# Fourth small expert in the mixture-of-experts stage of a two-layer decoder, and the order of its eight jobs

## The chip, the cores and the metric

The kernel runs on one core of a Trainium2 chip. Its engines are TensorE (PE in the profile; PEld is its weight load), VectorE (DVE), ScalarE (ACT), GpSimd (POOL) and SyncE (SP), each with its own instruction stream, joined by semaphores. The metric is the device time of one execution in microseconds (us); lower is better.

## The reference, cut to what matters

Two layers run on 256 tokens of 1024 numbers, all in float32. Layer 0 is retention and a dense SwiGLU, layer 1 is block attention and a top-2-of-8 mixture of experts (MoE). The change is in the MoE alone:

```python
def moe_swiglu(x, router, w_in, w_out):
    B, T, D = x.shape
    xt = x.reshape(B * T, D)
    logits = (xt @ router).astype(jnp.float32)
    top_v, top_i = lax.top_k(logits, MOE_TOP_K)
    top_w = jax.nn.softmax(top_v, axis=-1)
    gates = jnp.sum(jax.nn.one_hot(top_i, N_EXPERTS, dtype=jnp.float32) * top_w[..., None], axis=1)
    out = jnp.zeros_like(xt)
    for e in range(N_EXPERTS):
        out = out + gates[:, e:e + 1].astype(x.dtype) * swiglu(xt, w_in[e], w_out[e])
    return out.reshape(B, T, D)
```

Each expert has an input matrix of 1024 x 7168 (gate and up halves of 3584) and an output matrix of 3584 x 1024, in all 42 MB of 1024 x 1024 bytes. With the reference's inputs, its router gives experts 0 to 7 the following numbers of tokens: 60, 61, 58, 57, 89, 66, 54, 67 (sum 512).

## The kernel before

A float32 product is made of products of a high part and a low part (float32r, a shorter mantissa): x = hi + lo. ACT writes the high part of each weight tile (`moe_hi`, L834), DVE subtracts it from the tile and writes the low part (`moe_lo`, whose subtraction is L964 of `lo_of`), and PE multiplies.

The MoE works in eight **jobs**, one an expert, and each job in 42 **units** of 1 MB of weights (128 partitions x 2048 numbers). SP loads the units in order into eight buffers (six of `raw`, two of `more_raw`), a load waiting until `moe_lo` of eight units earlier is done (L498). ACT and DVE write the two parts into four buffer pairs (`whi`/`wlo` three, `whi_more`/`wlo_more` one), each waiting until PE has used the unit of four earlier. ACT and DVE programs are written out by hand, four units ahead of PE's: `moe_hi(n+4)`, `moe_lo(n+4)` stand in the turn of unit n, beside the activations and copies of that turn.

A job first needs its tokens. They are gathered by a product of h with a 0/1 matrix `sel` (made on POOL, `select`), and the result is added back with the transposed matrix (`turn_sel` at unit 6 of a job; `scatter` at units 2 and 4 of the next job, after which DVE adds it into h, L1323). There are two forms of a job:

- **Big** (`big_unit`): up to 128 tokens. The tokens' hi and lo parts are two separate stationary operands of 128 columns (`xg_big`), and each weight tile is swept three times: hi x hi, hi x lo, lo x hi (L1422, L1423, L1424). A unit has 12 matmuls of 512 columns.
- **Small** (`small_unit`): up to 64 tokens. The hi and lo parts of 64 tokens stand side by side in one stationary operand of 128 columns (`xg_small`), and each tile is swept twice: with the hi weights and with the lo weights (L1842, L1843). A unit has 8 matmuls of 512 columns. The two halves are added by a product with `merge` (L1879, `turn_merged`), and there are row copies on ACT (L860, L865).

Expert 0 is always first. The other seven are sorted by their number of tokens, from most to least, and get positions 1 to 7 (`sort_experts`). `POSITION` says which position runs as which job. Positions 5, 6 and 7 are small, so the forms of jobs 0 to 7 are big, small, big, small, big, small, big, big. The tokens of jobs 2m+1 and 2m+2 are gathered together in job 2m, in eight steps (`gather_pair`, units 13 to 31; a step is four matmuls, L1759), each copied by ACT before the next (`copy_gathered`). Job 6 gathers for job 7 alone.

If an expert has more tokens than its capacity (128 for a big one, 64 for a small one), `see_excess` sets `over`, and after the eight jobs eight more big jobs run for the rest (`more > 0`).

POOL loads the last norm's parameters (`ln_last`, 2 x 512 KB) when the last unit of job 6 is used (L619). After the last job, `drain_y`, `scatter`, the two adds into h and the last layer norm end the kernel.

Of the kernel before, what the change touches and what calls it, by code (L numbers as in the profile page):

```python
# [7 lines left out]
ACT = mybir.ActivationFunctionType  # L8
# [6 lines left out]
P = 128  # L15
# [14 lines left out]
def build(nc, x, ln_g, ln_b, ret_w_in, ret_gn_g, ret_gn_b, ret_w_out, kv_w, moba_w_q, moba_w_out,  # L30
# [3 lines left out]
    KD = D // P  # L34
# [10 lines left out]
    EX = moe_router.shape[2]  # L45
# [14 lines left out]
    JOBS = EX  # L60
# [8 lines left out]
    assert EFF == 3 * W + BANK and len(BIG_STREAM) == len(SMALL_STREAM) == JOB_UNITS and U_MOE % SPLIT == 0 and JOB_UNITS % RAW == 0  # L69

    HALF = P // 2
    POSITION = [0, 5, 1, 6, 2, 7, 3, 4]
    SMALL = [position >= 5 for position in POSITION]
    BIGS, SMALLS = SMALL.count(False), SMALL.count(True)
    CAPACITY = [P] * 5 + [HALF] * 3
    FIRST_KEY = 1 << 14
    assert not SMALL[0] and not SMALL[-1]

    BIG_SILU = {3: (0, 0), 4: (0, 1), 11: (1, 0), 12: (1, 1), 23: (2, 0), 24: (2, 1), 33: (3, 0)}
    BIG_MUL = {7: (0, 0), 8: (0, 1), 19: (1, 0), 20: (1, 1), 31: (2, 0), 32: (2, 1), 35: (3, 0)}  # L80
# [37 lines left out]
    with ctx:  # L118
        def sem(name):
            return ctx.enter_context(nc.semaphore(name))  # L120
# [4 lines left out]
        def place(name, shape, dt=F32, at=None):  # L125

            size = (math.prod(shape[1:]) * 4 + 31) // 32 * 32
            line = ALIGN if size >= ALIGN else 32
            start = (map_at[0] + line - 1) // line * line if at is None else at
            assert start + size <= nc.sbuf_usable_end, name  # L130
            if at is None:
                map_at[0] = start + size
            return nc.alloc_sbuf_tensor_at(name, shape, dt, offset=start), start
# [46 lines left out]
        capacity, _ = place("capacity", [P, EX])  # L180
        key_limit, _ = place("key_limit", [P, EX])
# [21 lines left out]
        xg_big = [place(f"xg_big{i}", [P, KD, 2, P], F32R, at=xT_at + i * 8192)[0] for i in range(2)]  # L203
# [3 lines left out]
        xg_small, _ = place("xg_small", [P, KD, P], F32R)  # L207
# [11 lines left out]
        sel, _ = place("sel", [P, 2, T, 2 * P], F32R)  # L219
# [25 lines left out]
        ps = ctx.enter_context(nc.psum_tensor("ps", [P, 8, BANK], F32))  # L245
# [66 lines left out]
        moe_tables = sem("moe_tables")  # L312
# [8 lines left out]
        gathered = sem("gathered")  # L321
        big_copied = sem("big_copied")
        small_copied = sem("small_copied")
# [108 lines left out]
        def bigs_before(j):  # L432
            return SMALL[:j].count(False)

        def smalls_before(j):
            return SMALL[:j].count(True)

        def sel_of(j):

            if j == 0:  # L440
                return sel[:, 1, :, 0:P]
            c = P if SMALL[j] else 0
            return sel[:, (j - 1) // 2 % 2, :, c:c + P]
# [4 lines left out]
        def _(sp):  # L448
# [47 lines left out]
            def moe_unit(u, i, e, slot, dst, free, small=False):  # L496
                src, rows = moe_source(i, e, small)
                sp.wait_ge(lo_done, free)  # L498
                sp.dma_start(dst.rearrange("p (k n) -> p k n", k=rows), src).then_inc(landed[slot], 16)

            def expert(position):
                return sp.value_load(expert_at[0:1, position:position + 1].bitcast(I32), min_val=0, max_val=EX - 1)

            for j in range(JOBS):
                if j == 0:
                    e = 0
                else:
                    if j == 1:
                        sp.wait_ge(experts_sorted, 1)
                    e = expert(POSITION[j])  # L510
                for i in range(JOB_UNITS):
                    n = j * JOB_UNITS + i
                    if n == RAW:
                        sp.wait_ge(h_ready, T * 2 + 1)
                    back = MRAW if n >= MRAW else RAW
                    moe_unit(U_MOE + n, i, e, moe_slot(n), moe_raw(n), U_MOE + n - back + 1 if n < RAW or n >= MRAW else U_MOE,
                             SMALL[j])

# [17 lines left out]
        def _(pool):  # L536
# [49 lines left out]
            for t in range(T):  # L586
# [4 lines left out]
            pool.tensor_tensor(merge[:, :], ident[:, 0:HALF], ident[:, HALF:P], ALU.add).then_inc(moe_tables, 1)  # L591
            pool.iota(key_low[:, :], pattern=[[-1, EX]], base=EX - 1, channel_multiplier=0,
                      allow_small_or_imprecise_dtypes=True).then_inc(moe_tables, 1)
            pool.memset(capacity[:, 0:5], float(P)).then_inc(moe_tables, 1)
            pool.memset(capacity[:, 5:EX], float(HALF)).then_inc(moe_tables, 1)
            pool.memset(key_limit[:, 0:1], float(FIRST_KEY + EX * (P + 1))).then_inc(moe_tables, 1)
            pool.memset(key_limit[:, 1:5], float(EX * (P + 1))).then_inc(moe_tables, 1)
            pool.memset(key_limit[:, 5:EX], float(EX * (HALF + 1))).then_inc(moe_tables, 1)
            pool.wait_ge(moe_tables, 8)
            pool.memset(key_low[:, 0:1], float(FIRST_KEY + EX - 1)).then_inc(moe_tables, 1)  # L600
            for n in (1, 2):
# [11 lines left out]
            for q in range(4):  # L613
                if q >= 1:
                    pool.wait_ge(selT_done, 2 * q - 1)
                for t in range(T):
                    for j in range(2 * q + 1, min(2 * q + 3, JOBS)):
                        select(q, t, SMALL[j], POSITION[j])
            pool.wait_ge(unit_used, first_unit(JOBS - 1))  # L619
# [4 lines left out]
        def _(act):  # L624
# [76 lines left out]
            for i in range(PIECES):  # L701
                w = slice(i * UNIT // PIECES, (i + 1) * UNIT // PIECES)
# [13 lines left out]
            for s in range(12):  # L716
                u, c = U_RET_IN + QK_UNITS + 4 + s, 2 + s // 2
# [172 lines left out]
            def copy_gathered(j, k):  # L890

                step = j // 2 * KD + k
                w = P if j + 2 >= JOBS else P + HALF
                src = ps[:, 7, 0:2 * w].rearrange("p (s n) -> p s n", s=2)
                act.wait_ge(gathered, step + 1)
                nc.scalar.activation(xg_big[(bigs_before(j) + 1) % 2][:, k, :, :], src[:, :, 0:P],
                                     ACT.Copy).then_inc(big_copied, 1)
                if w > P:
                    nc.scalar.activation(xg_small[:, k, :].rearrange("p (s n) -> p s n", s=2), src[:, :, P:w],
                                         ACT.Copy).then_inc(small_copied, 1)  # L900

            def drain_y(u):
                unit_done(act, u + JOB_UNITS - 1, 0)
# [30 lines left out]
            with act.If(more > 0):  # L934
                with act.Fori(0, JOBS) as p:
                    for k in range(KD):
                        act.wait_ge(gathered, 4 * KD + k + 1 + KD * p)
                        nc.scalar.activation(xg_big[0][:, k, :, :].rearrange("p s n -> p (s n)"), ps[:, 7, 0:2 * P],
                                             ACT.Copy).then_inc(big_copied, 1)
                    copy_selT(JOBS + p)  # L940
                    for i in range(AHEAD):
                        again_hi(p, i)
                    for i in range(JOB_UNITS):
                        again_hi(p, i + AHEAD)
                        big_drains(i, U_AGAIN + JOB_UNITS * p, BIGS + p)
                    drain_y(U_AGAIN + JOB_UNITS * p)
# [7 lines left out]
        def _(dve):  # L954
# [360 lines left out]
            def place_gates():  # L1315

                then(to_positions(gate_of[:, :, 1:1 + EX], gate_expert))
                then(nc.vector.tensor_copy(gate_of[:, :, 0:1], gate_of[:, :, 1 + POSITION[-1]:2 + POSITION[-1]]))

# [44 lines left out]
            for j in range(JOBS):  # L1364
                u = first_unit(j)
                for i in range(JOB_UNITS):
# [11 lines left out]
                    else:  # L1378
                        if i == 0:
                            drain_y(j - 1)  # L1380
                        elif i in (3, 5):
                            t, at = i // 5, 1 + POSITION[j - 1]
                            dve.wait_ge(h_scaled, T)
# [35 lines left out]
        def _(pe):  # L1419
# [335 lines left out]
            def gather_step(k, dst, chosen, w):  # L1755

                for s, src in enumerate((h_hi, h_lo)):
                    for t in range(T):
                        last = pe.matmul(dst[:, s * w:(s + 1) * w], src[:, t, k * P:(k + 1) * P], chosen[:, t, 0:w],  # L1759
                                         start=(t == 0), stop=(t == T - 1))  # L1760
                return last

            def gather_pair(j, k):

                w = P if j + 2 >= JOBS else P + HALF
                if k == 0:
                    pe.wait_ge(selT_ready, j + 1)
                    pe.wait_ge(sel_ready, min(2 * T * (j // 2 + 1), T * (JOBS - 1)))
                else:
                    pe.wait_ge(big_copied, j // 2 * KD + k)  # L1770
                    if w > P:
                        pe.wait_ge(small_copied, j // 2 * KD + k)
                gather_step(k, ps[:, 7, :], sel[:, j // 2 % 2], w).then_inc(gathered, 1)

            def turn_sel(job, chosen):

# [172 lines left out]
            with pe.If(more > 0):  # L1949
                with pe.Fori(0, JOBS) as p:  # L1950
                    pe.wait_ge(selT_ready, JOBS + p)
                    pe.wait_ge(y_lo_done, 2 * JOBS + 2 * p)
                    for t in range(T):
                        scatter(t)
                        pe.wait_ge(summed, T * (JOBS - 1) + t + 1 + T * p)
                    pe.wait_ge(sel_again, T + T * p)
                    for k in range(KD):
                        gather_step(k, ps[:, 7, :], sel[:, 0], P).then_inc(gathered, 1)
                        pe.wait_ge(big_copied, 4 * KD + k + 1 + KD * p)
                    turn_sel(JOBS + p, sel[:, 0, :, 0:P])  # L1960
                    big = BIGS + p
                    for i in range(JOB_UNITS):
                        big_unit(i, U_AGAIN + JOB_UNITS * p, big, JOBS + p, xg_big[0], whi[:, i % SPLIT, :],
                                 wlo[:, i % SPLIT, :], (big_silu, 7 * big),
                                 (big_mul, 7 * big))
                        big_turn(i, big)
# [26 lines left out]
```

## Time and profile before

| | |
|---|---|
| time, median of 3 runs | 1469.05 us (1467.59 to 1470.61) |
| the profiled execution | 1468.5 us |
| its span in the profile | 1466.7 us, so 1.8 us lie around the span |
| PE, DVE, ACT busy | 97%, 78%, 66% of the span |
| the MoE's eight jobs | from about 540 us to the end |

Each row of a grouped view tells a line of the code, the engine, the operation, output and inputs with shapes, the number of instructions, their busy time and mean duration, and the idle time ahead of them with what ended it. Matmuls overlap, so one of 0.39 us starts every 0.23 us; intervals between starts are what counts. In the view of busy time by stretch a row gives the stretch and its length in us, then busy time and number of instructions of PE, PEld, DVE, ACT and POOL, PE's granted clock (1.00 is full), the DMA engines' busy share and the rate in GB/s. In a row of a timeline stand start, duration, engine, line and operation, and in brackets the idle time before it and what ended it. In a row of DMA issues the last number is the median time from issue to landing in us.

### The profile page before, as it was taken

How to read it: one execution, taken by the hardware profiler on the slowest of the kernel's cores; microseconds unless marked ns; L12 is line 12 of the kernel's file. 1: busy time of each engine (PE TensorE's matmuls, PEld its weight loads, DVE VectorE, ACT ScalarE, POOL GpSimd, SP SyncE). 2: the span in 40 equal slices, each digit the busy share in tenths (PEclk: the TensorE clock that was granted, in tenths of full speed). 3: DMA queues.
4: the chain of work that ended last, by engine and by line, in shares of the span. 5: the costliest groups of instructions: out<-in, count | busy, mean ns of one | idle time of the engine just before them, and what ended most of it. 6: DMA issues, size and time to landing. Idle time of an engine off the chain costs nothing.

```text
span 1466.7 us, 18711 instructions
## 1 busy us (share of the span) xinstructions
PE 1423.2 (97%) x7478; PEld 1207.5 (82%) x7478; DVE 1142.5 (78%) x795; ACT 961.6 (66%) x796; POOL 55.7 (4%) x66
## 2 busy tenths in 40 slices
PE   9999999999999999999999999999999999999996
PEld 9987789999889887887778887778887778888885
DVE  5456564545556598899998888999888999889886
ACT  5334544343444477778987777987777997777774
POOL 2001200000000021000002000001000000000000
PEclk9999999999999999999999999999999999999999
DMA  9654556555564469999999999999999999999990
GB/s 361 214 172 149 202 173 209 187 182 190 172 202 147 136 249 364 359 355 370 417 420 420 377 358 346 404 420 420 382 357 351 395 420 420 398 358 379 378 343 30
DMA packets 158743, 446.89 MB, mean 305 GB/s; under 512 B 7088, under 2 KB 46000, under 8 KB 158656
## 3 DMA queue, kind: packets, MB, share of 16 engines
q1 hardware_dynamic: 156832, 439.38, 80.5%
q0 software_dynamic: 1824, 6.33, 1.2%
q8 instruction: 57, 0.93, 0.2%
q14 instruction: 30, 0.25, 0.0%
HBM read 444.63 MB, written 1.05 MB: 304 GB/s over the span
## 4 chain that ended last, share of the span: by engine, by line
PE 73%; DVE 22%; ACT 2%; issue 2%; POOL 0%; DVEq 0%; ACTq 0%; POOLq 0%
PE ps L1422 21%; PE ps L1424 21%; PE ps L1423 21%; DVE wlo L964 13%; DVE wlo_more L964 4%; PE ps L1842 1%; PE ps L1843 1%; PE ps L1836 1%; PE ps L1759 1%; ACT whi L834 1%; PE ps L1879 1%; DVE h L1323 1%; DVE wlo L387 1%; PE ps L1468 1%; DVE y_lo L964 1%
## 5 line engine op out<-in xcount | busy, mean ns | idle before, releaser
L964 DVE TENSOR_TENSOR wlo<-raw,whi 128x2048 fp32r<-128x2048 f32 (+1 forms) x214 | 480.0, 2257 | 53.6 <-ACT whi L834 52.9
L834 ACT ACTIVATE whi<-raw 128x2048 fp32r<-128x2048 f32 x208 | 397.3, 1917 | 104.2 <-PE ps L1424 95.8
L387 DVE TENSOR_TENSOR wlo<-raw,whi 128x2048 fp32r<-128x2048 f32 x80 | 184.1, 2302 | 154.8 <-ACT whi L380 154.8
L380 ACT ACTIVATE whi<-raw 128x2048 fp32r<-128x2048 f32 x82 | 156.8, 1912 | 152.4 <-PE ps L1424 151.3
L1422 PE MATMUL ps<-whi,xg_big 128*128 128x512 f32 x420 | 166.1, 395 | 0.5 <-DVE wlo L964 0.5
L1424 PE MATMUL ps<-whi,xg_big 128*128 128x512 f32 x420 | 163.9, 390 | 0.0
L1423 PE MATMUL ps<-wlo,xg_big 128*128 128x512 f32 x420 | 163.7, 390 | 0.0
L1422 PE MATMUL ps<-xT_hi,whi 128*128 128x256 f32 x576 | 163.3, 284 | 0.0
L1424 PE MATMUL ps<-xT_hi,wlo 128*128 128x256 f32 x576 | 163.0, 283 | 0.0
L1423 PE MATMUL ps<-xT_lo,whi 128*128 128x256 f32 x576 | 163.0, 283 | 0.0
L1422 PEld LDWEIGHTS ps<-xT_hi,whi 128*128 128x128 f32 x576 | 110.5, 192 | 0.5
L1423 PEld LDWEIGHTS ps<-xT_lo,whi 128*128 128x128 f32 x576 | 110.5, 192 | 0.4
L1424 PEld LDWEIGHTS ps<-xT_hi,wlo 128*128 128x128 f32 x576 | 110.5, 192 | 0.0
L964 DVE TENSOR_TENSOR wlo<-more_raw,whi 128x2048 fp32r<-128x2048 f32 x42 | 96.1, 2287 | 12.3 <-ACT whi L834 12.3
L1842 PE MATMUL ps<-whi,xg_small 128*128 128x512 f32 x252 | 99.7, 396 | 2.8 <-DVE wlo L964 2.3
L834 ACT ACTIVATE whi_more<-more_raw 128x2048 fp32r<-128x2048 f32 x42 | 80.6, 1918 | 32.9 <-PE ps L1424 20.8
L964 DVE TENSOR_TENSOR wlo_more<-more_raw,whi_more 128x2048 fp32r<-128x2048 f32 x42 | 96.0, 2286 | 7.5 <-ACT whi_more L834 7.2
L834 ACT ACTIVATE whi_more<-raw 128x2048 fp32r<-128x2048 f32 x42 | 80.5, 1917 | 31.3 <-PE ps L1424 20.7
L964 DVE TENSOR_TENSOR wlo_more<-raw,whi_more 128x2048 fp32r<-128x2048 f32 x42 | 96.0, 2287 | 6.0 <-ACT whi_more L834 6.0
L1843 PE MATMUL ps<-wlo,xg_small 128*128 128x512 f32 x252 | 98.3, 390 | 0.0
L834 ACT ACTIVATE whi<-more_raw 128x2048 fp32r<-128x2048 f32 x42 | 80.5, 1917 | 18.8 <-PE ps L1424 17.6
L1422 PEld LDWEIGHTS ps<-whi,xg_big 128*128 128x128 f32 x420 | 79.0, 188 | 16.7 <-issue 1.7
(253 smaller groups left out, 2750.7 us busy)
## 6 DMA issues: line engine op xcount, KB each, us to landing
raw<-in_moe_w_in SPq DMA_DIRECT2D x166, 1024.0 KB, 6.9
raw<-in_moe_w_out SPq DMA_DIRECT2D x86, 1024.0 KB, 7.8
more_raw<-in_moe_w_in SPq DMA_DIRECT2D x58, 1024.0 KB, 7.0
more_raw<-in_moe_w_out SPq DMA_DIRECT2D x26, 1024.0 KB, 7.7
raw<-in_ret_w_in SPq DMA_DIRECT2D x23, 1024.0 KB, 6.8
raw<-in_ffn_w_in SPq DMA_DIRECT2D x22, 1024.0 KB, 4.9
raw<-in_ffn_w_out SPq DMA_DIRECT2D x11, 1024.0 KB, 4.8
raw<-in_ret_w_out SPq DMA_DIRECT2D x8, 1024.0 KB, 4.9
```

Of the source, the lines that this page charges most:

```text
L380: nc.scalar.activation(whi[:, u % SPLIT, :], src, ACT.Copy).then_inc(hi_done, 1)
L387: nc.vector.tensor_tensor(wlo[:, u % SPLIT, :], src, whi[:, u % SPLIT, :].bitcast(F32), ALU.subtract).then_inc(lo_done, 1)
L834: nc.scalar.activation(moe_split(n)[0], moe_raw(n), ACT.Copy).then_inc(hi_done, 1)
L964: return nc.vector.tensor_tensor(dst, src, hi.bitcast(F32), ALU.subtract)
L1323: nc.vector.scalar_tensor_tensor(out=h[:, t, :], in0=ps[:, at:at + 2, :].rearrange("p b n -> p (b n)"), scalar=gate, in1=h[:, t, :], op0=A ...
L1422: pe.matmul(dst, a_hi, b_hi, start=start, stop=False, skip_group_check=True)
L1423: pe.matmul(dst, a_hi, b_lo, start=False, stop=False, skip_group_check=True)
L1424: return pe.matmul(dst, a_lo, b_hi, start=False, stop=stop, skip_group_check=True)
L1468: pe.matmul(ps[:, at, 3 * P:4 * P], ident[:, :], ident[:, :], start=True, stop=True)
L1759: last = pe.matmul(dst[:, s * w:(s + 1) * w], src[:, t, k * P:(k + 1) * P], chosen[:, t, 0:w], start=(t == 0), stop=(t == T - 1))
L1842: pe.matmul(dst, a, hi, start=start, stop=False, skip_group_check=True)
L1843: return pe.matmul(dst, a, lo, start=False, stop=stop, skip_group_check=True)
```

## The change

Four positions (4 to 7) are small instead of three, and the jobs alternate: `POSITION` is now 0, 4, 1, 5, 2, 6, 3, 7, so that the forms are big, small, big, small, big, small, big, small. Jobs 0 to 6 have the forms that they had; job 7 is now small. Job 1 takes the expert of position 4 instead of 5, job 3 that of 5 instead of 6, job 5 that of 6 instead of 7, and job 7 that of position 7 (the fewest tokens) instead of 4. The gather of job 6 is for 64 slots alone, and ACT copies it to `xg_small` alone; steps wait on `small_copied` only. The tables of capacities and limits follow, and the overflow jobs' constants too.

```diff
-    POSITION = [0, 5, 1, 6, 2, 7, 3, 4]
-    SMALL = [position >= 5 for position in POSITION]
+    POSITION = [0, 4, 1, 5, 2, 6, 3, 7]
+    FIRST_SMALL = 4
+    SMALL = [position >= FIRST_SMALL for position in POSITION]
     BIGS, SMALLS = SMALL.count(False), SMALL.count(True)
-    CAPACITY = [P] * 5 + [HALF] * 3
...
-            pool.memset(capacity[:, 0:5], float(P)).then_inc(moe_tables, 1)
-            pool.memset(capacity[:, 5:EX], float(HALF)).then_inc(moe_tables, 1)
+            pool.memset(capacity[:, 0:FIRST_SMALL], float(P)).then_inc(moe_tables, 1)
+            pool.memset(capacity[:, FIRST_SMALL:EX], float(HALF)).then_inc(moe_tables, 1)
...
             def copy_gathered(j, k):
                 step = j // 2 * KD + k
-                w = P if j + 2 >= JOBS else P + HALF
+                w = HALF if j + 2 >= JOBS else P + HALF
                 src = ps[:, 7, 0:2 * w].rearrange("p (s n) -> p s n", s=2)
                 act.wait_ge(gathered, step + 1)
-                nc.scalar.activation(xg_big[(bigs_before(j) + 1) % 2][:, k, :, :], src[:, :, 0:P],
-                                     ACT.Copy).then_inc(big_copied, 1)
-                if w > P:
-                    nc.scalar.activation(xg_small[:, k, :].rearrange("p (s n) -> p s n", s=2), src[:, :, P:w],
-                                         ACT.Copy).then_inc(small_copied, 1)
+                if w > HALF:
+                    nc.scalar.activation(xg_big[(bigs_before(j) + 1) % 2][:, k, :, :], src[:, :, 0:P],
+                                         ACT.Copy).then_inc(big_copied, 1)
+                nc.scalar.activation(xg_small[:, k, :].rearrange("p (s n) -> p s n", s=2), src[:, :, w - HALF:w],
+                                     ACT.Copy).then_inc(small_copied, 1)
...
             def gather_pair(j, k):
-                w = P if j + 2 >= JOBS else P + HALF
+                c, w = (P, HALF) if j + 2 >= JOBS else (0, P + HALF)
                 if k == 0:
                     pe.wait_ge(selT_ready, j + 1)
                     pe.wait_ge(sel_ready, min(2 * T * (j // 2 + 1), T * (JOBS - 1)))
                 else:
-                    pe.wait_ge(big_copied, j // 2 * KD + k)
-                    if w > P:
-                        pe.wait_ge(small_copied, j // 2 * KD + k)
-                gather_step(k, ps[:, 7, :], sel[:, j // 2 % 2], w).then_inc(gathered, 1)
+                    pe.wait_ge(small_copied, j // 2 * KD + k)
+                gather_step(k, ps[:, 7, :], sel[:, j // 2 % 2, :, c:c + w], w).then_inc(gathered, 1)
```

## Rows read from the trace of the kernel before

**Rows 1.** The page's first part: span, busy time by engine.
```profile
span 1466.7 us, 18711 instructions
PE 1423.2 (97%) x7478; PEld 1207.5 (82%) x7478; DVE 1142.5 (78%) x795; ACT 961.6 (66%) x796; POOL 55.7 (4%) x66
```
**Rows 2.** Timeline of PE: the transposes of `sel` (L1778) of jobs 1 to 7.
```profile
672.72 0.38 PE L1778 MATMUL ps<-ident,sel 128*128 128x128 f32 x2
...
775.09 0.38 PE L1778 MATMUL ps<-ident,sel 128*128 128x128 f32 x2
...
900.48 0.38 PE L1778 MATMUL ps<-ident,sel 128*128 128x128 f32 x2
...
1002.88 0.38 PE L1778 MATMUL ps<-ident,sel 128*128 128x128 f32 x2
...
1127.03 0.38 PE L1778 MATMUL ps<-ident,sel 128*128 128x128 f32 x2
...
1229.42 0.38 PE L1778 MATMUL ps<-ident,sel 128*128 128x128 f32 x2
...
1352.80 0.38 PE L1778 MATMUL ps<-ident,sel 128*128 128x128 f32 x2
```
**Rows 3.** Busy time by stretch (job 5, job 7): columns as told above.
```profile
1105.40:1207.30 101.90, 96.54 (x459) 77.21 (x457) 98.18 (x54) 89.36 (x67) 0.00 (x0) 0.98 1.01 390
...
1332.10:1451.80 119.70, 119.70 (x543) 98.69 (x541) 102.33 (x58) 82.72 (x56) 1.11 (x2) 1.00 0.79 301
```
**Rows 4.** Timeline of DVE: job 5's last low part, job 6's first.
```profile
1202.80 2.28 DVE L964 TENSOR_TENSOR wlo_more<-raw,whi_more 128x2048 fp32r<-128x2048 f32 x1
1205.00 4.48 DVE L964 TENSOR_TENSOR wlo<-raw,whi 128x2048 fp32r<-128x2048 f32 x2
```
**Rows 5.** Timeline of PE: last unit of job 5, end of job 7.
```profile
1205.13 0.50 PE L1842 MATMUL ps<-whi_more,gT_small 128*128 128x512 f32 x1
...
1206.86 0.39 PE L1843 MATMUL ps<-wlo_more,gT_small 128*128 128x512 f32 x1
...
1451.43 0.39 PE L1424 MATMUL ps<-whi_more,gT_lo 128*128 128x512 f32 x1
```
**Rows 6.** Timeline of PE: second scatters of jobs 1, 3, 5.
```profile
666.22 0.50 PE L1785 MATMUL ps<-y_hi,selT 128*128 128x512 f32 x1 [2.90 <-DVE h L1323]
...
891.15 0.80 PE L1785 MATMUL ps<-y_hi,selT 128*128 128x512 f32 x1 [2.89 <-DVE h L1323]
...
1118.96 0.64 PE L1785 MATMUL ps<-y_hi,selT 128*128 128x512 f32 x1 [2.89 <-DVE h L1323]
```
**Rows 7.** Chain that ended last: gather steps of jobs 4, 6.
```profile
1023.30 0.42 PE ps L1759 x4
1023.72 0.25 PE ps L1422
...
1249.84 0.40 PE ps L1759 x4
1250.23 0.28 PE ps L1422
```
**Rows 8.** DMA issues at 1120 to 1130, 1200 to 1210, 1333 us; last: landing.
```profile
raw<-in_moe_w_in SPq DMA_DIRECT2D x1, 1024.0 KB, 7.6
...
raw<-in_moe_w_in SPq DMA_DIRECT2D x5, 1024.0 KB, 12.4
...
ln_last<-in_ln_b POOLq DMA_DIRECT2D x1, 512.0 KB, 9.5
```
**Rows 9.** Busy time by stretch: two short stretches of job 5.
```profile
1130.00:1140.00 10.00, 10.00 (x53) 8.36 (x51) 9.24 (x6) 9.25 (x9) 0.00 (x0) 1.00 0.96 336
1190.00:1200.00 10.00, 9.46 (x40) 6.78 (x38) 10.00 (x7) 9.37 (x6) 0.00 (x0) 1.00 1.02 420
```
**Rows 10.** Timeline of ACT: job 5's last high part, job 6's second.
```profile
1198.15 1.90 ACT L834 ACTIVATE whi_more<-raw 128x2048 fp32r<-128x2048 f32 x1
...
1202.60 1.92 ACT L834 ACTIVATE whi<-raw 128x2048 fp32r<-128x2048 f32 x1 [0.28 <-DMA raw<-in_moe_w_in]
```

More of the change, by code:

```diff
@@ L71, in build @@
     HALF = P // 2
-    POSITION = [0, 5, 1, 6, 2, 7, 3, 4]
-    SMALL = [position >= 5 for position in POSITION]
+    POSITION = [0, 4, 1, 5, 2, 6, 3, 7]
+    FIRST_SMALL = 4
+    SMALL = [position >= FIRST_SMALL for position in POSITION]
     BIGS, SMALLS = SMALL.count(False), SMALL.count(True)
-    CAPACITY = [P] * 5 + [HALF] * 3
     FIRST_KEY = 1 << 14
-    assert not SMALL[0] and not SMALL[-1]
+    assert not SMALL[0] and SMALL[-1]
     BIG_SILU = {3: (0, 0), 4: (0, 1), 11: (1, 0), 12: (1, 1), 23: (2, 0), 24: (2, 1), 33: (3, 0)}
@@ L593, in _ @@
                       allow_small_or_imprecise_dtypes=True).then_inc(moe_tables, 1)
-            pool.memset(capacity[:, 0:5], float(P)).then_inc(moe_tables, 1)
-            pool.memset(capacity[:, 5:EX], float(HALF)).then_inc(moe_tables, 1)
+            pool.memset(capacity[:, 0:FIRST_SMALL], float(P)).then_inc(moe_tables, 1)
+            pool.memset(capacity[:, FIRST_SMALL:EX], float(HALF)).then_inc(moe_tables, 1)
             pool.memset(key_limit[:, 0:1], float(FIRST_KEY + EX * (P + 1))).then_inc(moe_tables, 1)
-            pool.memset(key_limit[:, 1:5], float(EX * (P + 1))).then_inc(moe_tables, 1)
-            pool.memset(key_limit[:, 5:EX], float(EX * (HALF + 1))).then_inc(moe_tables, 1)
+            pool.memset(key_limit[:, 1:FIRST_SMALL], float(EX * (P + 1))).then_inc(moe_tables, 1)
+            pool.memset(key_limit[:, FIRST_SMALL:EX], float(EX * (HALF + 1))).then_inc(moe_tables, 1)
             pool.wait_ge(moe_tables, 8)
@@ L936, in _ @@
                     for k in range(KD):
-                        act.wait_ge(gathered, 4 * KD + k + 1 + KD * p)
+                        act.wait_ge(gathered, JOBS // 2 * KD + k + 1 + KD * p)
                         nc.scalar.activation(xg_big[0][:, k, :, :].rearrange("p s n -> p (s n)"), ps[:, 7, 0:2 * P],
@@ L1958, in _ @@
                         gather_step(k, ps[:, 7, :], sel[:, 0], P).then_inc(gathered, 1)
-                        pe.wait_ge(big_copied, 4 * KD + k + 1 + KD * p)
+                        pe.wait_ge(big_copied, (BIGS - 1) * KD + k + 1 + KD * p)
                     turn_sel(JOBS + p, sel[:, 0, :, 0:P])
```

## The prediction

> **What bounds the kernel now.** I read the page's first part, then the busy time by stretch, then the timelines of PE and DVE at the ends of a small and of a big job. The first part gives PE as busy in 97% of the span [rows 1], which says little alone, since overlapping matmuls count as busy. The stretches tell the jobs apart. In job 7, which is big, PE is busy all of 119.7 us and DVE 102.3 of them: PE sets the pace [rows 3]. In job 5, which is small, DVE is busy 98.2 of 101.9 us and PE 96.5: DVE is the fuller engine [rows 3]. The end of job 5 shows it. DVE starts its last low part at 1202.80 and the next one at 1205.00, 2.20 us a unit, and PE starts the last unit at 1205.13, at once when that part is written; the eight matmuls' starts lie between 1205.13 and 1206.86, so PE needs about 2.0 us for a unit and waits for DVE [rows 4, 5]. So a small job is no third shorter, as its 8 matmuls for 12 would have it: it is cut off by the splitting of the weights. What it costs has to be read from the three small jobs that run already.
>
> The transposes of `sel` at unit 6 are the milestones [rows 2]. From a small job's to that of the big job behind it it is 102.37, 102.40 and 102.39 us (jobs 1, 3, 5). From a big job's to that of the small job behind it, it is 125.39 (job 2) and 124.15 us (job 4). From job 6 to job 7, big to big, it is 123.38 us.
>
> **The change part by part.** All is compared with the profiled run, whose span is 1466.7 us and whose time is 1.8 us more, 1468.5; that is 0.55 under the median of 1469.05.
>
> (a) Jobs 0 to 6, up to unit 6 of job 6 at 1229.42 us. Their forms, unit streams and gathers are the same, and which expert stands at a small position changes only addresses of loads and a column of `slot_of` and `gate_of`. The memsets of two tables have other widths on POOL, long before they are read. Price 0.
>
> (b) Job 7's own units. From its transpose to the start of its last matmul job 7 takes 1451.43 - 1352.80 = 98.63 us [rows 2, 5]. Job 5, small, takes 1206.86 - 1127.03 = 79.83 us for the same units [rows 2, 5]. Difference: -18.80 us. It may be carried over because in job 5 the low parts of the next job's units come behind the low part of unit 41 on DVE (the one of 1205.00 is job 6's first), so they delay nothing of job 5 itself; in the last job they are absent, and nothing else is in their place. The high part of unit 41 started at 1198.15, on ACT, 4.6 us before the low part needed it [rows 4, 10], so ACT doesn't set this end either.
>
> (c) The way into job 7. With a small job behind job 6 the interval from transpose to transpose is that of job 4 or 2, not 123.38 us. It falls in two. From the big job's transpose to the second scatter it is 116.06 us (775.09 to 891.15) and 116.08 us (1002.88 to 1118.96) [rows 2, 6], so it can be trusted. There PE waited 2.9 us for DVE's add into h, in all three small jobs, since DVE has low parts queued ahead of the add [rows 6]. From the scatter to the small job's transpose it is 6.50, 9.33 and 8.07 us in jobs 1, 3 and 5 [rows 2, 6]: the first matmul is at 0.50 us in job 1, and at 0.80 and 0.64 in the others, where PE's granted clock had fallen to its lower level, 1.2 GHz, for some matmuls after that wait. The way in is 116.07 plus one of the three: 122.57, 124.14 or 125.40 us. Against 123.38 that is -0.81, +0.76 or +2.02. I take the middle one, +0.8, as the value of the nearest small job in time, and keep both ends.
>
> (d) The gather of job 6. Its eight steps are four matmuls each, now of 64 columns instead of 128; jobs 0, 2 and 4, whose intervals I used in (c), have 192. With 192 columns a step takes 0.42 us and the matmul behind it 0.25; with 128 columns it takes 0.40 and 0.28 [rows 7], 0.67 and 0.68 in sum. A third fewer columns bring nothing, so the step is at a floor that the columns don't set. For 64 columns no row exists. Upper end: the same, 0. Lower end: halving from 128 in proportion to columns, -0.20 us a step or -1.6 us in all. I take 0, because the step from 192 to 128 brought 0. Copies on ACT in job 6: one to `xg_small` instead of one to `xg_big`, a smaller one; ACT is not what PE waits for in a big job (PE is busy without a gap in such a one [rows 3]), so 0. PE's new wait in steps 1 to 7 is for that copy on ACT instead of the bigger one; what is queued behind it on PE is the next unit, and the steps lie two units or more apart, 5 us, so it is met.
>
> (e) Moved with it: the load of `ln_last` (1 MB in all on POOL's queue), issued when job 6 ends. Until now it fell into a big job's slack, now it falls into a small job, where loads are issued at DVE's faster pace. In job 5 the loads took 7.6 us to land at its start and 12.4 at its end, and the rate rose from 336 to 420 GB/s [rows 8, 9]: they were falling behind. ACT first waited for a load at job 6's unit 1 (0.28 us, at 1202.60), two units behind the last of job 5's own [rows 10]. In the last job there is no unit behind unit 41, so this wait can't come. The extra 1 MB is 2.5 us at 420 GB/s; at the start the loads run 84 GB/s under that rate, which gives back 0.8 MB in each 10 us, so it should be taken in by 20 to 30 us into the job. Price 0, with an end of +2.5 us if it isn't. The landing itself (9.5 us for the second half [rows 8]) is needed only some 100 us later.
>
> (f) The end. `drain_y`, the scatters, the adds and the norm are as before: 1466.7 - 1451.43 = 15.27 us behind the start of the last matmul [rows 1, 5]. DVE and ACT are free at that point as before. Price 0.
>
> The Trainium skill holds something against all this. Its page "DMA: Bandwidth & Descriptors", section "Where 436 GB/s comes from", says that for transfers between HBM and SBUF the HBM side binds, at about 358 GB/s for a core. As an estimate from that page, a job's 44.04 MB would need 123 us, a small job could not be shorter than a big one, and the change would give nothing. The trace disagrees: job 5 ran at 390 GB/s over its whole length and at 420 in its last part [rows 3, 9].
>
> **The sum.** -18.8 (b) + 0.8 (c) = -18.0 us. The span becomes 1448.7 us, the time 1450.5; set against the median instead of the profiled run, 1451.05 us. I give 1451.0.
>
> **The rivals.**
> 1. *The load stream falls behind in the last job.* For it: landings stretch to 12.4 us in job 5, and 1 MB more is put into this one [rows 8]. Against it: job 5's own last high part met no late load [rows 10]. It gives the sum plus up to 2.5 us: 1453.5 us.
> 2. *A small job at the end is worth nothing*, because the stream or DVE needs as long for its 42 units as PE does for a big one. It would be so if a job's bytes could come no faster than in about 120 us; the price is the whole of (b), and the way in stays: about 1470 us. Against it: three small jobs that run in 102.4 us [rows 2], which include all their loads.
> 3. *Slower: the overflow runs.* Position 4 now has 64 slots instead of 128. From 65 tokens on at that position, eight more big jobs run. Each costs at least the big-to-big interval, 123.4 us [rows 2], in all some 990 us: about 2440 us. By the tokens of the reference's inputs expert 0 (60) is fixed, and the other seven in order are 89, 67, 66, 61, 58, 57, 54. Position 4 is the fourth of these, 61 tokens, three under the limit. So it decides only if the inputs were others, or if the kernel's arithmetic moved four tokens.
>
> **How the numbers follow.** Forecast 0.86, rival 1 0.10, rival 2 0.02, rival 3 0.02. Range: down from 1451.0 by 1.6 (a way in without a fallen clock) and by 1.6 (gathers by columns), not quite both, 1448; up by 1.3 (a longer fall of the clock) and 2.5 (rival 1), and a little for the spread of runs (3 us between the three of before), 1455. Rivals 2 and 3 stay outside with 0.04. Forecast and rival 1 are both faster by more than 0.2% (2.9 us, about what a measurement of this kernel can tell from no change): faster 0.96, same 0.02, slower 0.02.
>
> **What would show it.** Right: transposes of jobs 1 to 6 at the same times within 3 us; job 6 to job 7 at 122 to 126 us; from job 7's transpose to its last matmul 79.8 us; 15.3 us behind that; DVE, not PE, full in job 7; gather steps in job 6 at 0.4 us. Rival 1 would show waits of `whi` for a DMA inside job 7, and the 79.8 us stretched to 82. The forecast is wrong if the 79.8 us depend on something of job 6's that I took as idle, or if job 7 meets a wait that jobs 1, 3 and 5 don't have.

## The result, and the profile after

The changed kernel takes 1450.27 us (median of 4 runs, 1448.69 to 1451.99), the kernel before 1469.83 us (4 runs); the ratio is 0.9869, 95% interval 0.9854 to 0.9884. So the change gives 1.3%, some 19 us. The four runs fall into two pairs, 1448.7 and 1448.9 against 1451.6 and 1452.0 us, and the median lies between them; a difference of a microsecond or two between two such medians says little. The profiled execution is the one of 1448.69 us; its page begins:

```profile
span 1447.0 us, 18516 instructions
PE 1397.1 (97%) x7394; PEld 1183.1 (82%) x7394; DVE 1135.3 (78%) x789; ACT 962.1 (66%) x804; POOL 54.6 (4%) x66
```

The shares of the engines are those of before [rows 1], which shows how little they tell: 19.7 us are gone and no share has moved. The milestones do tell. Here is the timeline of PE of the changed kernel, the transposes of `sel` of jobs 1 to 7 (L1776 is what was L1778), answering [rows 2]:

```profile
671.76 0.38 PE L1776 MATMUL ps<-ident,sel 128*128 128x128 f32 x2
...
774.19 0.38 PE L1776 MATMUL ps<-ident,sel 128*128 128x128 f32 x2
...
899.52 0.38 PE L1776 MATMUL ps<-ident,sel 128*128 128x128 f32 x2
...
1001.90 0.38 PE L1776 MATMUL ps<-ident,sel 128*128 128x128 f32 x2
...
1126.02 0.38 PE L1776 MATMUL ps<-ident,sel 128*128 128x128 f32 x2
...
1228.42 0.38 PE L1776 MATMUL ps<-ident,sel 128*128 128x128 f32 x2
...
1351.10 0.38 PE L1776 MATMUL ps<-ident,sel 128*128 128x128 f32 x2
```

Up to job 6 the intervals are within 0.1 us of those of before (102.43, 125.33, 102.38, 124.12, 102.40), though jobs 1, 3 and 5 now run other experts. These milestones lie about 1 us earlier, and so does the transpose of job 0 (547.31 against 548.22 us): this came ahead of the jobs, where nothing was changed. Now the end of job 7: PE's last unit and first scatter, DVE's last low part, and ACT's last high part, answering [rows 5, 4, 10]:

```profile
1429.21 0.50 PE L1840 MATMUL ps<-whi_more,gT_small 128*128 128x512 f32 x1
...
1430.92 0.39 PE L1841 MATMUL ps<-wlo_more,gT_small 128*128 128x512 f32 x1
1434.18 0.49 PE L1783 MATMUL ps<-y_hi,selT 128*128 128x512 f32 x1 [2.87 <-DVE y_lo L964]
```
```profile
1426.86 2.29 DVE L964 TENSOR_TENSOR wlo_more<-more_raw,whi_more 128x2048 fp32r<-128x2048 f32 x1
```
```profile
1422.71 1.92 ACT L834 ACTIVATE whi_more<-more_raw 128x2048 fp32r<-128x2048 f32 x1 [0.38 <-DMA more_raw<-in_moe_w_out]
```

PE starts the last unit when DVE has written its low part, as it did in job 5. The sum of the differences between the two traces:

| part | before, us | after, us | difference |
|---|---|---|---|
| up to job 6's transpose | 1229.42 | 1228.42 | -1.00 |
| job 6's transpose to job 7's | 123.38 | 122.68 | -0.70 |
| job 7's transpose to its last matmul | 98.63 | 79.82 | -18.81 |
| behind the start of the last matmul | 15.27 | 16.08 | +0.81 |
| span | 1466.7 | 1447.0 | -19.7 |

### The profile page after: what moved, and what is told of

It is laid out like the page before. It is cut to its first block, busy times and chain, and to the rows that moved or that the text cites. A ratio compares the mean times of both kernels' runs of the same rounds, so it can differ in the third digit from the quotient of the medians.

```text
span 1447.0 us, 18516 instructions
## 1 busy us (share of the span) xinstructions
PE 1397.1 (97%) x7394; PEld 1183.1 (82%) x7394; DVE 1135.3 (78%) x789; ACT 962.1 (66%) x804; POOL 54.6 (4%) x66
## 4 chain that ended last, share of the span: by engine, by line
PE 67%; DVE 27%; ACT 3%; issue 2%; POOL 0%; DVEq 0%; ACTq 0%; POOLq 0%
PE ps L1422 19%; PE ps L1424 19%; PE ps L1423 19%; DVE wlo L964 17%; DVE wlo_more L964 5%; PE ps L1840 2%; PE ps L1841 2%; ACT whi L834 1%; PE ps L1877 1%; PE ps L1759 1%; PE ps L1834 1%; DVE h L1323 1%; DVE y_lo L964 1%; DVE wlo L387 1%; DVE gT_small L964 1%
## 5 line engine op out<-in xcount | busy, mean ns | idle before, releaser
L1840 PE MATMUL ps<-whi,xg_small 128*128 128x512 f32 x336 | 133.0, 396 | 3.8 <-DVE wlo L964 3.1
L1422 PE MATMUL ps<-whi,xg_big 128*128 128x512 f32 x336 | 133.3, 397 | 0.6 <-DVE wlo L964 0.6
L1424 PE MATMUL ps<-whi,xg_big 128*128 128x512 f32 x336 | 131.1, 390 | 0.0
L1841 PE MATMUL ps<-wlo,xg_small 128*128 128x512 f32 x336 | 131.0, 390 | 0.0
L1423 PE MATMUL ps<-wlo,xg_big 128*128 128x512 f32 x336 | 131.0, 390 | 0.0
L1422 PE MATMUL ps<-whi,xT_hi 128*128 128x512 f32 (+1 forms) x224 | 85.3, 381 | 2.4 <-DVE wlo L387 2.2
```

Of the source, the lines that this page charges most:

```text
L1422: pe.matmul(dst, a_hi, b_hi, start=start, stop=False, skip_group_check=True)
L1423: pe.matmul(dst, a_hi, b_lo, start=False, stop=False, skip_group_check=True)
L1424: return pe.matmul(dst, a_lo, b_hi, start=False, stop=stop, skip_group_check=True)
L1840: pe.matmul(dst, a, hi, start=start, stop=False, skip_group_check=True)
L1841: return pe.matmul(dst, a, lo, start=False, stop=stop, skip_group_check=True)
```

## The experiments

Each kernel below is the changed kernel with the edit shown, where nothing else is said. "To the end of job 7" means from its transpose to the start of its last matmul.

**What sets the pace of the small last job: DVE, ACT or the loads?** Two kernels halve one thing each in job 7: DVE's subtractions in the first, the loads in the second. ACT's work was not halved.

```diff
                     dve.wait_ge(hi_done, U_MOE + n + 1)
-                    lo_of(lo, moe_raw(n), hi).then_inc(lo_done, 1)
+                    w = UNIT // 2 if n >= (JOBS - 1) * JOB_UNITS else UNIT
+                    lo_of(lo[:, 0:w], moe_raw(n)[:, 0:w], hi[:, 0:w]).then_inc(lo_done, 1)
```

> In job 7 DVE writes only the first half of the columns of each low part (the other half keeps old numbers), so each subtraction is halved from 2.2 to 1.1 us. Part of the computation is left out. Theory (DVE sets the small job's pace): from job 7's transpose to its last matmul the 79.8 us fall, down to what comes next: ACT, 37 high parts by 1.8 us and its copies, some 75 us; time 1445 to 1447 us. Rival (loads set the pace): 79.8 us as before.

```diff
-                sp.dma_start(dst.rearrange("p (k n) -> p k n", k=rows), src).then_inc(landed[slot], 16)
+                k = rows // 2 if U_MOE + (JOBS - 1) * JOB_UNITS <= u < U_AGAIN else rows
+                sp.dma_start(dst.rearrange("p (k n) -> p k n", k=rows)[:, 0:k, :], src[:, 0:k, :]).then_inc(landed[slot], 16)
```

> In job 7 each load brings half of its bytes (the other half of the buffer keeps old numbers). Part of the computation is left out. Theory (DVE sets the pace): from job 7's transpose to its last matmul 79.8 us, no wait for a DMA in job 7, time 1450 us. Rival (loads set the pace): clearly under 79.8 us, by 2 us or more.

Busy time by stretch, from the transpose to about the last matmul, of the changed kernel, of the one with half subtractions, and of the one with half loads (columns as ahead of the prediction: PE, PEld, DVE, ACT, POOL, clock, DMA share, GB/s):

```profile
1351.10:1431.00 79.90, 77.75 (x379) 62.45 (x377) 76.25 (x41) 68.35 (x52) 0.00 (x0) 1.00 0.89 355
```
```profile
1349.50:1426.50 77.00, 75.89 (x379) 62.85 (x377) 43.44 (x40) 68.55 (x52) 0.00 (x0) 1.00 0.94 381
```
```profile
1354.00:1434.00 80.00, 77.81 (x379) 62.46 (x377) 75.90 (x41) 68.22 (x52) 0.00 (x0) 1.00 0.54 165
```

Each of the two ran once. With half the bytes, 165 GB/s instead of 355, the job took 79.82 us to its end, just as before. So the loads set nothing in it. With half subtractions it took 76.93 us, and the profiled run was 1444.6 us. DVE is then busy 43.4 of 77 us and, by its waits, idle for 32.0 us because of ACT's high parts:

```profile
DVE wlo L964 <- ACT whi L834: 24.5, 22, 2.4
DVE wlo_more L964 <- ACT whi_more L834: 7.5, 8, 1.3
```

So DVE does set the small job's pace, but only by 2.9 us in 80: when half of it goes, ACT comes next, and ACT itself then waits 1.5 + 1.2 us for PE and 3.4 us for loads. Which of the three would hold the job at 76.9 us isn't shown, since both halvings at once and a halving of ACT's work weren't tried. In the changed kernel DVE is not free of ACT either: in the same stretch it waits 1.7 us for high parts. The kernel with half subtractions had its transpose of job 7 at 1349.51, 120.22 us behind job 6's: with the first low parts shorter, DVE came earlier to its add into h, and PE's wait there was 0.93 us instead of 2.89. That wait is looked at below.

**Do more bytes at its start delay the last job?** The load of `ln_last` was doubled; DVE's wait for it was raised from 32 to 64.

```diff
             load_ln(3)
+            pool.wait_ge(ln_landed[3], 32)
+            load_ln(3)
```

> The load of ln_last (1 MB) is made twice, one behind the other, at the start of job 7; the rest is the changed kernel. Theory (the small last job is set by DVE, loads have room): from job 7's transpose to its last matmul 79.8 us as in the changed kernel, the one 0.38 us wait of ACT for a load becomes longer, time 1450 us. Rival (the load stream sets job 7's pace, so that its bytes count): 1 MB more costs 2.5 us at 420 GB/s, 82.3 us and 1453 us.

The time was 1451.87 us (ratio to before 0.988, 0.986 to 0.9899); to the end of job 7 it was 79.82 us, in spite of four waits of ACT for a load instead of one. The timeline of ACT of this kernel shows them:

```profile
1419.40 1.92 ACT L836 ACTIVATE whi<-raw 128x2048 fp32r<-128x2048 f32 x1 [0.46 <-DMA raw<-in_moe_w_out]
1421.90 1.92 ACT L836 ACTIVATE whi<-raw 128x2048 fp32r<-128x2048 f32 x1 [0.58 <-DMA raw<-in_moe_w_out]
1424.44 1.92 ACT L836 ACTIVATE whi<-more_raw 128x2048 fp32r<-128x2048 f32 x1 [0.31 <-DMA more_raw<-in_moe_w_out]
1426.91 1.92 ACT L836 ACTIVATE whi_more<-more_raw 128x2048 fp32r<-128x2048 f32 x1 [0.56 <-DMA more_raw<-in_moe_w_out]
```

So the extra bytes are met by ACT's lead over DVE and end there. One more megabyte doesn't reach DVE. The 1.6 us between this median and the changed kernel's don't come from job 7: in the profiled run the transpose of job 0 was 3.2 us later already (550.46 against 547.31 us), and from there to the last matmul the two traces agree within 0.1 us.

**Does the narrower gather bring anything?** Here job 6 gathers with 192 columns, as jobs 0, 2 and 4 do.

```diff
-                c, w = (P, HALF) if j + 2 >= JOBS else (0, P + HALF)
+                c, w = 0, P + HALF
```

(in `copy_gathered` `w` is `P + HALF` too, and only `xg_small` is written in job 6)

> The gather of job 6 is made with all 192 columns, as in jobs 0, 2 and 4; ACT copies the last 64 of them to xg_small, and nothing of the result changes. Theory (a step is at a floor that columns don't set): the interval from the transpose of job 6 to that of job 7 is within 0.5 us of the changed kernel's 122.68 us if the clock doesn't fall in job 7's start; time 1450 us, 0.9869 of before. Rival (a step costs by columns): eight steps with 128 columns more, 32 matmuls by some 0.05 us each, 1.7 us more in that interval.

The time was 1450.67 us (ratio 0.9871, 0.9851 to 0.9891), and job 6's transpose to job 7's took 122.56 us against 122.68: no difference. The chain of the changed kernel shows the step with 64 columns and the matmul behind it, then the wide kernel's, answering [rows 7]:

```profile
1248.84 0.37 PE ps L1759 x4
1249.21 0.31 PE ps L1422
```
```profile
1250.14 0.42 PE ps L1759 x4
1250.57 0.25 PE ps L1422
```

They take 0.68 and 0.67 us together; with 128 columns it was 0.68. A step costs the same with 64, 128 and 192 columns.

**Where do the 0.8 us behind the last matmul come from?** In the changed kernel the scatter started 0.90 us after DVE's last `y_lo`, in the kernel before 0.12 us. Between the last unit and the scatter PE reads the overflow flag and branches. These kernels have no such part in PE's program, once in the changed kernel, once in the kernel before:

```diff
-            pe.wait_ge(over_ready, 1)
-            more = pe.value_load(over[0:1, 0:1], min_val=0, max_val=1)
-            with pe.If(more > 0):
...
-            jobs = JOBS * more
+            jobs = 0
```

> PE's program has no overflow part, and so neither reads the flag nor branches behind the last job; the other engines keep theirs. Nothing of the result changes. In the changed kernel 16.08 us lie behind the start of the last matmul, 15.27 in the kernel before. Theory (PE, which waited for DVE's last low part, comes to its read and branch later and is late for the scatter): 15.2 us or less. Rival (the 0.8 us are of another cause): 16.1 us.

> The same removal of PE's overflow part from the kernel before the change. Nothing of the result changes. Theory (there PE's program had run ahead of its matmuls, so read and branch were hidden): 15.27 us behind the start of the last matmul as before, within 0.15. Rival (read and branch always cost): shorter by 0.8 us as in the changed kernel.

Each ran once. Behind the start of the last matmul lay 15.23 us in the first and 15.26 us in the second, against 16.08 and 15.27 with the overflow part. The chains that ended last, of the changed kernel, then of the first of these, between `y_lo` and the scatter:

```profile
1433.03 0.25 DVE y_lo L964
1433.28 0.90 issue
1434.18 0.49 PE ps L1783
```
```profile
1433.57 0.25 DVE y_lo L964
1433.82 0.04 issue
1433.87 0.50 PE ps L1783
```

So reading and branching cost 0.8 us in these two executions behind the small last job, and nothing behind the big one. The size is not fixed. In the other traces that end with a small job and the reading behind it, this gap was 0.92 (wide gather), 0.68 (the next experiment's kernel), 0.57 (`ln_last` twice), 0.54 (half loads) and 0.51 us (half subtractions), against 0.04 without the part; what sets it between 0.5 and 0.9 stays open. That the big last job hides the cost because PE's program runs ahead of its matmuls, while behind the small job PE has just waited for DVE, is the reading that fits; the traces show the effect and not the run-ahead, and the overflow kernel further on limits it.

**Is the way into a small job PE's own path, and what does the wait of 2.9 us cost?** In every small job PE waits at unit 4 for DVE's add into h [rows 6], which stands behind the low part of unit 6 in DVE's program. This kernel moves it ahead of that.

```diff
-                        elif i in (3, 5):
+                        elif i in ((2, 5) if SMALL[j] else (3, 5)):
```

> In the small jobs DVE adds the first half of the last job's result into h one turn earlier, before the low part of unit 6 instead of behind it; the rest is the changed kernel. It takes away the 2.9 us for which PE waits at a small job's unit 4. Theory (the way into a small job is PE's, so that wait and the fall of the clock behind it are on the path): the intervals from a big job's transpose to the small one's fall from 124.4, 125.3, 124.1 and 122.7 us to some 120 to 122, the intervals behind them stay at 102.4 and 79.8; some 10 us less than the changed kernel, 1440 us. Rival (DVE's low parts, one of which comes 1.2 us later, set the small job from its start): the intervals behind grow by what the ones ahead lose, time within 2 us of 1450.

1443.54 us, ratio 0.9828 (0.9814 to 0.9841). Big to small took 123.55, 121.66, 121.68 and 121.78 us instead of 124.45, 125.33, 124.12 and 122.68, 7.9 us less in all, and the intervals behind stayed (102.47 to 102.49, and 79.88). By the medians it is 6.7 us less than the changed kernel. So the theory holds and its rival doesn't, but 10 us was too much: of the 2.9 us, 0.7 stay, and 1.2 come back as a wait at unit 6, for DVE's second add. That leaves 0.9 us a job, which is all that jobs 1 and 7 gained. In job 5 of this kernel, timeline of PE:

```profile
1111.81 0.50 PE L1783 MATMUL ps<-y_hi,selT 128*128 128x512 f32 x1 [0.69 <-DVE h L1323]
...
1119.61 0.44 PE L1776 MATMUL ps<-ident,sel 128*128 128x128 f32 x2 [1.15 <-DVE h L1323]
```

The second scatters no longer start at a fallen clock: 0.50 us in all four small jobs, against 0.80 and 0.64 in [rows 6]. The rest of the gain comes from there. The largest single part, 3.7 us, is in job 3's start, where the clock had been low longest, and 2.4 us are in job 5's.

**What does the overflow cost?** The limit for small positions was set to 61 tokens, the number that the expert at position 4 has.

```diff
-            pool.memset(key_limit[:, FIRST_SMALL:EX], float(EX * (HALF + 1))).then_inc(moe_tables, 1)
+            pool.memset(key_limit[:, FIRST_SMALL:EX], float(EX * 61)).then_inc(moe_tables, 1)
```

> The changed kernel with the limit at which a position of a small job counts as too full set to 61 tokens instead of 65; position 4 has 61, so the eight overflow jobs run, with nothing to add. The result stays the same. By rival 3 of the prediction they cost at least 8 x 123.4 us, some 990 us: time about 2440 us. If no run of them came, position 4 would have fewer than 61 tokens: 1450 us.

2624.54 us: the eight jobs ran, so position 4 has 61 tokens or more and, as the changed kernel without them shows, no more than 64. They cost some 1175 us, not 990. The timeline of PE shows the transposes of two of them, 146.8 us apart:

```profile
1455.02 0.69 PE L1776 MATMUL ps<-ident,sel 128*128 128x128 f32 x2 [0.47 <-ACT xg_big L938]
...
1601.83 0.69 PE L1776 MATMUL ps<-ident,sel 128*128 128x128 f32 x2 [0.47 <-ACT xg_big L938]
```

That is 23 us more than a big job that overlaps with its neighbours: each gathers, scatters and waits by itself, and PE's granted clock was 0.90 on average from 1450 to 1600 us. How the 23 us divide among these isn't shown.

**A version that takes both costs away.** PE reads the flag at the start of job 7 and only branches behind it; the add is early in the small jobs (first kernel), or in all (second: `elif i in (2, 5)`).

```diff
                 for i in range(JOB_UNITS):
+                    if j == JOBS - 1 and i == 1:
+                        pe.wait_ge(over_ready, 1)
+                        more = pe.value_load(over[0:1, 0:1], min_val=0, max_val=1)
...
-            pe.wait_ge(over_ready, 1)
-            more = pe.value_load(over[0:1, 0:1], min_val=0, max_val=1)
             with pe.If(more > 0):
```

> The changed kernel with the earlier add of the small jobs, and PE reads the overflow flag at the start of job 7 instead of behind its last unit; the branch stays where it is. Theory (both costs are taken away, each on its own): intervals as with the earlier add alone, some 121.7 us into a small job and 79.9 to the end, and 15.3 us behind the last matmul, or somewhat more if the branch itself costs and not the reading; time 1442 to 1443 us. Rival (the branch costs, not the reading): 15.9 to 16.1 us behind the last matmul.

> The same, with the add one turn earlier in the big jobs too. There PE waits 0.7 us for it. Theory (the add comes as late in a big job as in a small one, behind one low part too many): the three intervals from a small job's transpose to the big one's fall from 102.4 to some 101.7 us, 2 us in all. Rival (a big job is late for another cause, and the low part behind the add is missed later): 102.4 us or more.

The first: 1441.12 us, ratio 0.980 (0.9784 to 0.9817). Its trace is of the slowest of its five executions, 1448.67 us, in which job 0's transpose came only at 556.55 us; the other four lie between 1440.1 and 1441.4 us. The kernel before took 1470.72 us beside it and 1468.51 beside the kernel with the early add alone, so the step between the two ratios, 0.9828 and 0.980, is within the noise. The gap ahead of the scatter was 0.12 us, and job 6's transpose to job 7's took 121.78 us as without the earlier reading, so the earlier reading takes the cost away and costs nothing at its new place. Yet 15.87 us lay behind the last matmul, because in this run the scatter met the lower clock: 0.43 us from matmul to matmul instead of 0.23, as its chain shows:

```profile
1433.39 0.12 issue
1433.51 0.49 PE ps L1783
1434.00 0.43 PE ps L1784
1434.43 0.43 PE ps L1783
```

The second: 1437.91 us, ratio 0.978 (0.9763 to 0.9796), the fastest kernel here, with a gap of 0.21 us ahead of the scatter and 15.31 us at the end. Small to big fell from 102.45 to 102.48 us to 101.56 and 101.57, 2.7 us in all, somewhat more than the 0.7 us each of the wait.

It doesn't follow that the reading costs and the branch doesn't. The kernel of the overflow experiment reads the flag behind the last unit, as the changed kernel does, and PE has waited for DVE there too; but its branch leads into the loop of eight jobs and not over it. Its chain:

```profile
1435.38 0.25 DVE y_lo L964
1435.63 0.04 issue
1435.67 0.50 PE ps L1783
```

The gap is 0.04 us, as without reading and branch. So the late reading alone costs nothing (this trace), and the branch over the loop with an early reading costs 0.2 us at most (0.12 and 0.21 us). Only the two together left 0.5 to 0.9 us; why stays open.

## Why the prediction was right

The time was forecast at 1451.0 us in a range of 1448 to 1455 and is 1450.27. The mechanism was right: nearly all of the gain, 18.8 us, is job 7's own stretch in the small form. That the sum came within 0.7 us is partly luck, since two terms missed with opposite signs and the median stands between two pairs of runs. Step by step, against the table of the first section:

- (a) Jobs 0 to 6 untouched: right. The intervals agree within 0.1 us. The 1 us ahead of them came before job 0's transpose; in the traces of the changed kernel and its variants that transpose lies anywhere from 547.3 to 556.6 us.
- (b) -18.80 us from two rows of another small job: measured -18.81. It was right to take the stretch from job 5 and not to work it out from matmul counts. A third less of the 98.63 us would have been 66; the half subtractions show why that isn't reached, since even with DVE's share halved the job stands at 76.9 us.
- (c) +0.8 us, the middle of -0.81, +0.76 and +2.02: measured -0.70. The choice was off by 1.5 us, the ends held. What decides is the clock behind the 2.9 us wait. The busy time by stretch of the changed kernel, from the second scatter to the transpose in jobs 3, 5 and 7, has the granted clock in its third column from the end:

```profile
890.25:899.50 9.25, 9.25 (x36) 7.71 (x37) 7.26 (x4) 2.51 (x3) 0.00 (x0) 0.68 1.00 381
1117.97:1126.00 8.03, 8.03 (x36) 6.74 (x37) 6.93 (x4) 2.41 (x3) 0.00 (x0) 0.79 1.03 384
1344.60:1351.10 6.50, 6.50 (x36) 5.60 (x37) 6.50 (x4) 2.43 (x3) 0.00 (x0) 1.00 1.03 418
```

  In one execution of the kernel with half loads (whose jobs before the last are untouched) the second scatters of jobs 3, 5 and 7 start so:

```profile
893.10 0.50 PE L1784 MATMUL ps<-y_hi,selT 128*128 128x512 f32 x1 [2.89 <-DVE h L1324]
...
1118.07 0.80 PE L1784 MATMUL ps<-y_hi,selT 128*128 128x512 f32 x1 [2.89 <-DVE h L1324]
...
1345.95 0.75 PE L1784 MATMUL ps<-y_hi,selT 128*128 128x512 f32 x1 [2.89 <-DVE h L1324]
```

  There the intervals were 122.57, 125.38 and 124.27 us, for jobs 3, 5 and 7, where the kernel before had 125.39 and 124.15 for jobs 3 and 5. The same wait in the same job meets the lower clock in one execution and not in the next. But the values are not free of one another. In all nine traces with these waits one job has the stretch of some 9.3 us and the next small job the one of 8.1, and the other small jobs have 6.5: jobs 3 and 5 in seven traces, jobs 5 and 7 in this one, job 5 alone (the 9.3) in the kernel before without PE's overflow part, which has no small job behind it. Job 7, where it is small and has this wait, got the full clock in five of six traces. So "the nearest small job" was no reason for +0.8, and the row of the kernel before, 6.50, 9.33, 8.07, shows the same order; what starts it in job 3 or in job 5 stays open. With four small jobs the order changes little in sum: the three intervals add up to 372.1 us in the changed kernel and 372.2 us here.
- (d) Gather 0: right, 122.56 against 122.68 us. The step that 192 to 128 columns brought nothing carried over to 64.
- (e) `ln_last` 0: right, and right for more than it: twice the bytes cost nothing. But that such a wait for a load "can't come" in the last job was wrong. ACT waited 0.38 us for the very last load. The prediction named such a wait as the sign of rival 1; it isn't, as long as DVE is behind anyway. The sign is the 79.8 us, and they stood.
- (f) The end at 0: wrong by 0.8 us. It looked at DVE and ACT and said of them that they are free; PE's own reading of the flag and its branch over the overflow part were put at nothing without a reason. Behind the big job they had cost nothing; behind a small one they left a gap of 0.5 to 0.9 us in six traces.
- The two misses, -1.5 and +0.8 us, and the 1 us of spread make up the difference between the -18.0 us forecast and the -19.7 us of the traces.

Of the rivals, 1 is refuted for this size by the doubled load, and 2 by the time and by the halved loads. The prediction had set a rule of the Trainium skill beside this, "DMA: Bandwidth & Descriptors", section "Where 436 GB/s comes from": the HBM side binds at some 358 GB/s for a core. It doesn't hold in this case, where one core runs: the loads moved 381 GB/s over the whole 77 us of the kernel with half subtractions. Rival 3 has the point from which it decides (the flag set at 61 tokens) and a price that was too low: some 1175 us for 990.

## What to carry to other kernels

When a unit of work is replaced by a form that runs elsewhere in the same program, read the whole stretch between two milestones from there; the ratio of instruction counts would have been wrong by 14 us here. Then look at what the faster form may uncover: here PE's register read and branch, which had cost nothing behind the big job. And when a job starts with a wait of PE for a small operation, look at what stands ahead of that operation in the other engine's program: the same low part moved behind the add in four small jobs was worth 7.9 us in the traces, and the same in three big jobs 2.7 more.

## What the runs showed of the hardware

- A gather step, four matmuls with their weight loads, takes 0.67 to 0.68 us together with the matmul behind it, at 64, 128 and 192 columns alike (full clock).
- The granted clock after one and the same 2.89 us wait of PE is full in some executions and at the lower level, 1.2 GHz, in others (0.50 against 0.80 us for the first matmul); between them lie 2.8 us in one job's start. Behind waits of 0.7 us at the same place, in the traces with the earlier add, the first matmul always took 0.50 us.
- A read of a flag into a PE register and a branch over a loop behind it left 0.5 to 0.9 us between DVE's last part and PE's scatter behind a small last job (six traces), against 0.04 us without them; behind a big one it was 0.12. With the reading made earlier it was 0.12 and 0.21, and with the late reading and the branch into the loop 0.04.
- Loads of 1 MB each ran at 381 GB/s over 77 us with one core at work, and at 420 over 10 us [rows 9].
